# A new order for a two-layer decoder trunk: two DMA queues of unequal shares in the planner, and blocks of 4, 3, 4, 3, 3 tiles

## The chip, the cores and the metric

The kernel runs on the eight cores of one Trainium2 chip. Every core reads all weights from HBM and computes one of eight prompts (2048 tokens) and 16 of 128 sample sequences (8 tokens each, 128 rows); the cores don't talk to each other. The metric is the device time of the slowest core in microseconds (us), the median of several executions. TensorE is called PE in the profile's rows, VectorE DVE, ScalarE ACT, GpSimd POOL, SyncE SP.

## The reference, cut to what matters

```python
def mixer_block(h, ...):                      # both layers
    hn = rms_norm(h, norm_mix)
    proj = hn @ w_in                          # (tokens, 7696)
    q, k, v, g_out, g_lr, xp, u, vv, gates = split(proj)
    g_log = log_sigmoid(g_lr @ w_gk2 + b_gk) / 16        # g_lr has 16 columns
    o, s_new = gla_mix(q, k, v, g_log, s_gla, chunk)     # per head: S = diag(a) S + k^T v, o = q S
    o = rms_norm(o, gla_norm) * silu(g_out)
    branch_a = o @ w_br_a
    pool_out, new_hist = pool_mix(xp, pool_hist, n_prev, w_pool_mix, pool_scale)
    branch_b = pool_out @ w_br_b
    branch_c = spatial_gate(gelu(u), gelu(vv), w_spatial, b_spatial) @ w_br_c
    ga, gb, gc = split(sigmoid(gates))
    return h + (ga * branch_a + gb * branch_b + gc * branch_c) @ w_out, s_new, new_hist, gelu(vv)

def ffn_block(h, ...):
    a = relu(rms_norm(h, norm_ffn) @ w_ff1)
    return h + (a * a) @ w_ff2
```

Model width is 1024, there are 4 heads with keys of 128 and values of 256, the feed-forward width is 4096, and there are two layers. Prompts start from empty states, samples from given ones.

## The kernel before, in words

A core's 2176 rows are 17 tiles of 128 tokens: tile 0 holds the samples, tiles 1 to 16 the prompt. `BLK` groups the tiles into five blocks of 3, 3, 3, 4 and 4. Products that put features on the partitions (k, q, the gates, the first feed-forward matrix) run once for a block, with 384 or 512 columns a matmul, and so need the normed rows of all tiles of their block; v and the second feed-forward matrix run tile by tile. The normed and transposed rows of all tiles stay in SBUF as `hn`.

A layer has these stages: `gla_project` (v, k, q and the low-rank gate, whose 16 columns come from the small matrix `wglr` and go through `wgk2`), `gla_gate` (silu of g_out) and `gla_scan` (the recurrence, tile by tile) for each block; `gla_sample`, the same for 32 pairs of sample and head pair, a generator that stops after certain numbers of them and goes on after the next block; `mix_block` (pooling and spatial gating); `gate_block`, in two halves of the features; `out_block`; and the feed-forward part in four slices, `ff1` and `ff2`. Ahead of the first layer the rows of x are loaded through three buffers `xt`, normed on ScalarE and VectorE, transposed by TensorE and copied to `hn`. The x loads of tiles 6 and up wait until slot 4 of the weight ring has landed (that is the chunk g0).

Weights pass through a ring of seven slots of 8 KB a partition, in the order v0, v1, k, q, g0, g1, xp, u, vv and so on. Each chunk is read as float32 and written as bfloat16 by a DMA on POOL's queue (line 675); the first two chunks, v0 and v1, come in two halves each (line 379), so that TensorE can start on 256 columns. POOL's queue also carries `wglr`, `wgk2` (wgk_bf in the rows), `wpm` and `wsT`. All other transfers (x, states, the vector constants, `bsp` and `rep`, spills and outputs) go through SyncE's queue. Both queues are served by the same 16 DMA engines.

The order of the work on each engine isn't that of the program's text. Every operation is recorded as a node with its reads and writes, an estimated time and latency; `lay_out` then simulates the five engines, the PSUM banks and the two DMA queues, and always takes the node that can start first (by rank where several can). The order that it finds is issued as it stands: an engine that waits on a node waits with all that is queued behind it. So an estimated landing time places matmuls, and it does so blindly. Scan nodes get a lower rank, `LIFT`, which brings them forward. Since helpers record every operation, nearly all matmuls have line 454 (transposes 467), ScalarE's work line 417 and VectorE's lines 425, 428 and 437.

The end of the kernel is `ff2` on the last block, and the last tile's norm and store in halves.

Of the kernel before, what the change touches and what calls it, by code (L numbers as in the profile page):

```python
# [12 lines left out]
KT = 8  # L13
SEQ = 2048
DEPTH = 2
# [8 lines left out]
BLK = [(0, 3), (3, 3), (6, 3), (9, 4), (13, 4)]  # L24
# [122 lines left out]
def build_program():  # L147
# [18 lines left out]
    w_glr = din("w_glr", [DEPTH, 128, KT, 16])  # L166
# [80 lines left out]
    def lay_out(seed):  # L247
# [18 lines left out]
        dma_at = [4000.0] * 5  # L266
# [4 lines left out]
        for _ in range(len(nodes)):  # L271
# [3 lines left out]
            for e in range(5):  # L275
                f = free[e]
                pick = None
                for n in ready[e]:
                    s = rdy[n.idx]
                    if s < f:  # L280
                        s = f
                    if pick is not None and s > pick[0][0] and s > f + 30.0:
                        continue
                    bk = None
                    for b in n.tiles:
                        if kof[id(b)] is None:
                            can = [k for k in b.allowed if bank_of[k] is None]
                            if not can or (len(can) < 2 and b is not tiles_in_order[oldest]):
                                bk = -1
                                break  # L290
                            bk = min(can, key=lambda k: bank_at[k])
                            if bank_at[bk] > s:
                                s = bank_at[bk]
                            break
                    if bk == -1:
                        continue
                    c0 = max(s, f + 30.0)
                    key = key_of[n.idx]
                    if e == 1 and n.aset is not None and n.aset != aset:
                        key += 60  # L300
                        c0 += swap
                    c = (c0, key)
                    if pick is None or c < pick[0]:
                        pick = (c, s, n, bk)
                if pick is not None and (best is None or pick[1] < best[1]):
                    best = pick
            assert best is not None, "no node can be placed"
# [9 lines left out]
            if n.byts:  # L317
                at0 = max(dma_at[e], s + occ)
                other = dma_at[7 - e]
                work = n.byts / (290.0 if e == 3 else 150.0 if dma_at[4] < 20000.0 else 245.0)  # L320
                both = max(0.0, other - at0)
                dma_at[e] = at0 + (both + work - both / 2 if work > both / 2 else work * 2)
                fin = dma_at[e] + (3500.0 if e == 3 else 2500.0)
# [13 lines left out]
            for m in n.succ:  # L337
                j = m.idx
                t = fin + 250.0 if e != 0 or m.E is not PE else fin - n.lat
                if t > rdy[j]:  # L340
                    rdy[j] = t
                need[j] -= 1
                if need[j] == 0:
                    ready[num[id(m.E)]].append(m)
# [17 lines left out]
    class DmaQ:  # L362
# [6 lines left out]
        def dma(self, out, in_, reads=(), writes=(), after=(), turn=False):  # L369
# [15 lines left out]
            if turn:  # L385
                n *= 3
            record(self.E, fn, reads, writes, 500.0 if self.E is SP else 900.0, 0.0, byts=n, after=after)
# [159 lines left out]
    mkb = [24, 30, 36, 42, 50]  # L547
# [103 lines left out]
    def wload(n):  # L651
# [26 lines left out]
        record(POOL, fn, (), [b] + (first[2 * k:2 * k + 2] if n in (NSLOT, NSLOT + 1) else []), 900.0 * len(todo), 0.0, byts=byts)  # L678
# [10 lines left out]
    def setup():  # L689
# [4 lines left out]
        memset(wglr.t[:, :, :], 0.0, [wglr])  # L694
# [18 lines left out]
    def gla_consts(l):  # L713
        plq.dma(wglr.t[:, :, 0:16], w_glr[l], writes=[wglr])
        plq.dma(wgk2.t[:, :], w_gk2[l], writes=[wgk2])

    def mix_consts(l):
        plq.dma(wpm.t[:, :, :], w_pmT[l].rearrange("g d c -> d g c"), writes=[wpm])
        for g in range(4):
            ts(wpm.t[:, g, :], wpm.t[:, g, :], vec_t.t[:, V_PSC + l * 4 + g:V_PSC + l * 4 + g + 1], ALU.mult, [wpm, vec_t], [wpm])  # L720
        spq.dma(bsp.t[:, :, :], b_sp[l:l + 1].broadcast_to([128, 4, 128]), writes=[bsp], after=[slots[6]])

    def mix_prep(l):
        plq.dma(wsT.t[:, :, :], w_spT[l].rearrange("g s t -> s g t"), writes=[wsT], after=[slots[6]])
        spq.dma(rep.t[:, :], rep_d[l], writes=[rep], after=[slots[6]])
# [220 lines left out]
    def gla_sample(l):  # L946
# [11 lines left out]
        for hp in range(2):  # L958
# [8 lines left out]
            for i in range(NSEQ_S):  # L967
# [22 lines left out]
                if n in (5, 15, 25):  # L990
                    yield
# [103 lines left out]
    def gate_block(l, hf, b):  # L1095
# [4 lines left out]
        if b == 0:  # L1100
            for g in range(4):
                ps = psum()
                pe_group([(ps.t[:, :], wpm.t[:, g, :], bbc[1][:, g, :], True, True)], [wpm, bbc[0]], [ps])
                act(bbc[1][:, g, :], ps.t[:, :], AF.Copy, [ps], [bbc[0]])
        for pi, (gw, sw, vw, ktn, src, k0) in enumerate(((ga, ba[0], ba[1], KT, hs, 0), (gb, bbc[0], bbc[1], 4, os_, 0), (gc, bbc[0], bbc[2], 4, os_, 4))):
            for m4 in range(4):
                m = hf * 4 + m4
                psg = hn_fm(b, gw[0], gw[1], m4 * 128)
# [25 lines left out]
    def out_block(l, b):  # L1134
# [8 lines left out]
        for t in tiles(b):  # L1143
            norm_to_hn(t, hB[t].t[:, :], hH[t], hj, hx[t % 2], turn=b >= 2)
# [33 lines left out]
    for t in range(NTILE):  # L1178
        if t == 6:
            wget(0, "g1")  # L1180
        spq.dma(xt[t % 3].t[:, :], rows(x_p, x_s, t), writes=[xt[t % 3]], after=[slots[4]] if t > 5 else ())
        if t == 0:
# [8 lines left out]
            wget(0, "v0")  # L1191
# [113 lines left out]
```

How the kernel before makes its waits and increments, by code:

```python
    def wait(self, tok):  # L43
        if tok is None:
            return
        sem, val = tok
        if sem is self.sem and self.name == "pe":
            return
        k = id(sem)
        if self.seen.get(k, 0) >= val:
            return
        self.e.wait_ge(sem, val)
        self.seen[k] = val
# [1 line left out]
    def tok(self, inst):  # L55
        self.cnt += 1
        inst.then_inc(self.sem, 1)
        return (self.sem, self.cnt)
# [311 lines left out]
            def fn(rs, ws, lt):  # L370
                k = self.i % len(self.sems)
                self.i += 1
                sem = self.sems[k]
                if self.cnt[k] > 0:
                    self.E.wait((sem, 16 * self.cnt[k]))
                acquire(self.E, rs, ws)
                for b in after:
                    self.E.wait(b.w)
                (self.E.e.dma_start_transpose(out=out, in_=in_) if turn else self.E.e.dma_start(out=out, in_=in_)).then_inc(sem, 16)
                self.cnt[k] += 1
                release((sem, 16 * self.cnt[k]), rs, ws)
# [290 lines left out]
        def fn(rs, ws, lt):  # L672
            acquire(POOL, rs, ws)
            for view, src in todo:
                nc.gpsimd.dma_start(out=view, in_=src).then_inc(slot_sem[k], 16)
                slot_cnt[k] += 1
            release((slot_sem[k], 16 * slot_cnt[k]), rs, ws)
```

## Time and profile before

| | |
|---|---|
| time, median of 3 runs | 2383.77 us (2382.52 to 2385.54) |
| the profiled execution's own time | 2381.28 us |
| its span on the slowest core (core 5) | 2380.2 us |
| spans of the eight cores | 2371.6 to 2380.2 us |
| granted TensorE clock, mean | 0.998 |
| TensorE busy | 2323.0 us (98%) |
| VectorE, ScalarE, GpSimd busy | 1273.8, 886.3, 245.9 us |
| DMA moved | 229.41 MB |

The span runs from the first instruction to the last. Busy time of TensorE is modelled for its pipelined matmuls; what is not busy is time in which it had nothing to do. A granted clock of 1.00 is 2.4 GHz, one of 0.50 is 1.2 GHz.

### The profile page before, as it was taken

What the parts mean: (1) busy time and instruction counts of PE and PEld (TensorE: products, weight loads), DVE (VectorE), ACT (ScalarE), POOL (GpSimd) and SP (SyncE); (2) the same over time, 40 slices, a digit from 0 to 9 for tenths busy, and PEclk for the clock granted to TensorE, in tenths of its full rate; (3) what the DMA queues carried; (4) which work ended last, traced back from release to release, by engine and by line L of the source; (5) the groups of instructions that cost most, each with busy time, mean ns of one, the idle gap of its engine ahead of it and who ended that gap; (6) DMA issues with size and microseconds to landing.
All of it is one profiled execution on the core that took longest, in us unless ns stands there. A gap on an engine that the chain in (4) does not pass through costs nothing.

```text
span 2380.2 us, 40912 instructions; the slowest of 8 cores (2371.6 to 2380.2 us)
## 1 busy us (share of the span) xinstructions
PE 2323.0 (98%) x13392; PEld 1236.5 (52%) x13392; DVE 1273.8 (54%) x2231; ACT 886.3 (37%) x1810; POOL 245.9 (10%) x266
## 2 busy tenths in 40 slices
PE   6899999999999999999999999999999999999998
PEld 4576555546445454545455555564554454545453
DVE  3787776444465444434567776744434644434355
ACT  3877753222233121212456678322222421211133
POOL 2123222000000000000012233200000000000000
PEclk9999999999999999999999999999999999999999
DMA  9554936154186040406492467451815642222112
GB/s 162 143 165 122 186 125 142 71 97 111 70 159 103 1 72 1 76 1 116 127 164 74 149 137 157 100 135 63 142 72 107 126 65 36 36 37 36 18 59 93
DMA packets 219415, 229.41 MB, mean 96 GB/s; under 512 B 54315, under 2 KB 203307, under 8 KB 216106
## 3 DMA queue, kind: packets, MB, share of 16 engines
q0 software_dynamic: 83584, 78.45, 23.8%
q1 hardware_dynamic: 135626, 148.35, 20.9%
q8 instruction: 113, 1.85, 0.3%
q14 instruction: 92, 0.75, 0.1%
HBM read 240.41 MB, written 55.05 MB: 124 GB/s over the span
## 4 chain that ended last, share of the span: by engine, by line
PE 91%; DVE 3%; issue 2%; ACT 2%; DMA 2%; POOL 0%; DVEq 0%; ACTq 0%; SPq 0%; POOLq 0%
PE ps L454 90%; DMA wring<-w_in 1%; PE ps L467 1%; DVE U L428 0%; DMA Sf<-sgla 0%; DVE Sf L428 0%; ACT rsg L417 0%; DVE tmp L428 0%; ACT L417 0%; ACT tmp L417 0%; DVE sqg L425 0%; DVE lv L815 0%; ACT Sb L417 0%; DVE pt L425 0%; ACT xj L417 0%
## 5 line engine op out<-in xcount | busy, mean ns | idle before, releaser
L454 PE MATMUL ps<-hn,wring 128*128 128x384 bf16 (+1 forms) x6400 | 1245.4, 347 | 7.8 <-DVE sgt L425 1.7
L454 PEld LDWEIGHTS ps<-hn,wring 128*128 128x128 bf16 x6400 | 621.6, 98 | 545.4 <-issue 13.4
L454 PE MATMUL ps<-wring,a 128*128 128x512 bf16 x2176 | 476.0, 379 | 0.2 <-DVE a L425 0.2
L417 ACT ACTIVATE rl<-ps 128x384 f32<-128x384 f32 (+1 forms) x320 | 169.9, 532 | 637.9 <-PE ps L454 522.2
L425 DVE TENSOR_TENSOR h<-h,ps 128x512 f32<-128x512 f32 x340 | 233.1, 687 | 277.1 <-PE ps L454 276.1
L454 PEld LDWEIGHTS ps<-wring,a 128*128 128x128 bf16 x2176 | 212.8, 98 | 255.1 <-issue 0.7
L425 DVE TENSOR_TENSOR a<-rl 128x384 bf16<-128x384 f32 (+1 forms) x320 | 194.9, 612 | 276.0 <-ACT rl L417 268.0
L417 ACT ACTIVATE sg<-ps 128x384 f32<-128x384 f32 (+1 forms) x240 | 127.9, 533 | 450.3 <-PE ps L454 322.3
L454 PE MATMUL ps<-wring,hn 128*128 128x256 bf16 (+1 forms) x1088 | 193.7, 330 | 12.2 <-DMA wring<-w_in 10.8
L425 DVE TENSOR_TENSOR tmp<-sg,ps 128x384 f32<-128x384 f32 (+1 forms) x160 | 97.3, 608 | 154.4 <-ACT sg L417 79.1
L454 PEld LDWEIGHTS ps<-wring,hn 128*128 128x128 bf16 x1088 | 105.2, 99 | 79.3 <-issue 15.3
L454 PE MATMUL ps<-OBs,wring 128*128 128x384 bf16 (+1 forms) x640 | 143.8, 347 | 0.0
L675 POOL DMA_DIRECT2D wring<-w_ff x32 | 28.0, 875 | 1047.2 <-PE ps L454 1047.2
L425 DVE TENSOR_TENSOR acc<-sg,ps 128x384 f32<-128x384 f32 (+1 forms) x80 | 48.5, 607 | 162.7 <-PE ps L454 162.7
L454 PE MATMUL ps<-H4s,wring 128*128 128x384 bf16 (+1 forms) x640 | 130.7, 347 | 0.0
L454 PE MATMUL ps<-wring,mg 128*128 128x512 bf16 x544 | 119.7, 379 | 0.0
L425 POOL TENSOR_TENSOR go<-tmp,go 128x512 bf16<-128x512 f32 x64 | 77.8, 1221 | 244.4 <-DVE tmp L428 213.0
L417 ACT ACT_TABLE_LOAD x71 | 91.1, 1283 | 26.4 <-PE ps L454 24.2
L454 PEld LDWEIGHTS ps<-H4s,wring 128*128 128x128 bf16 x640 | 62.5, 98 | 55.7 <-issue 0.3
L454 PEld LDWEIGHTS ps<-OBs,wring 128*128 128x128 bf16 x640 | 62.6, 98 | 55.0
L454 PEld LDWEIGHTS ps<-wring,mg 128*128 128x128 bf16 x544 | 52.8, 98 | 61.3
L428 DVE SCALAR_TENSOR_TENSOR tmp<-ps,vec_t,rsg 128x256 f32<-128x256 f32 x136 | 61.7, 477 | 28.6 <-ACT rsg L417 27.5
(137 smaller groups left out, 1777.6 us busy)
## 6 DMA issues: line engine op xcount, KB each, us to landing
wring<-w_ff POOLq DMA_DIRECT2D x32, 1024.0 KB, 13.1
wring<-w_in POOLq DMA_DIRECT2D x28, 1024.0 KB, 16.1
Sf<-sgla SPq DMA_DIRECT2D x64, 256.0 KB, 3.7
gla_s<-Sf SPq DMA_DIRECT2D x64, 256.0 KB, 2.8
H4s<-H_d SPq DMA_DIRECT2D x12, 768.0 KB, 8.5
OBs<-OB_d SPq DMA_DIRECT2D x12, 768.0 KB, 5.0
h_d<-h SPq DMA_DIRECT2D x17, 512.0 KB, 2.7
h<-h_d SPq DMA_DIRECT2D x17, 512.0 KB, 9.9
```

Source lines behind the costliest of these rows:

```text
L417: op(ACT, lambda: nc.scalar.activation(out=now(out), in_=now(in_), func=func, **kw), reads, writes, occ, 125.0, SETS.get(func))
L425: op(E, lambda: E.e.tensor_tensor(out=now(out), in0=now(in0), in1=now(in1), op=alu), reads, writes, occ, 90.0)
L428: op(DVE, lambda: nc.vector.scalar_tensor_tensor(out=now(out), in0=now(in0), scalar=scalar, in1=now(in1), op0=op0, op1=op1), reads, writes ...
L454: inst = nc.tensor.matmul(now(m[0]), m[1], m[2], start=m[3], stop=m[4], **kw)
L467: inst = nc.tensor.transpose(now(o), i, ident_ap)
L675: nc.gpsimd.dma_start(out=view, in_=src).then_inc(slot_sem[k], 16)
```

## The change

The planner's DMA model: before, one finishing time for each queue, with fixed rates and a rough rule for overlap. Now the two queues are simulated as they run. A transfer joins its queue when it is issued, needs its bytes over 300 (SyncE) or 265 (POOL) bytes per ns plus 100 ns, and goes 3 or 1.5 times slower while the other queue has something to move; 2000 ns after its end it has landed, and only then its users become ready. DMA transposes count their bytes once, and take the queue's engine longer.

The data: `wglr` comes from the host padded to 32 columns, so that neither the memset nor the strided write is needed. `wglr` and `wgk2` of the first layer are recorded after v1, not after v0. `bsp` and `rep` wait for the norm of tile 5 (before: for slot 6's last load, which does not exist yet in the first layer, so that they were loaded at once). The x loads wait for slot 4 from tile 7 on, and g1 is requested at tile 7. Blocks are 4, 3, 4, 3, 3 tiles. The sample generator stops after 8, 18 and 28 pairs, before after 6, 16 and 26. The four products that fuse the pooling map into its branch matrix stand two by two ahead of the third and fourth feature tile of the first gated product, before all four ahead of the first. The merged rows `mg` move in SBUF with the block sizes. In `out_block` the tiles from 6 on go through DMA transposes, as before.

```diff
-BLK = [(0, 3), (3, 3), (6, 3), (9, 4), (13, 4)]
+BLK = [(0, 4), (4, 3), (7, 4), (11, 3), (14, 3)]
...
-    w_glr = din("w_glr", [DEPTH, 128, KT, 16])
+    w_glr = din("w_glr", [DEPTH, 128, KT, 32])
...
+            upto = best[1] if best is not None else 1e12
+            while clock < upto and (coming or moving[3] or moving[4]):
+                on = [(moving[3], 3.0 if moving[4] else 1.0), (moving[4], 1.5 if moving[3] else 1.0)]
+                on = [(q, r) for q, r in on if q]
+                to = min([upto] + [clock + q[0][1] * r for q, r in on] + ([max(clock, coming[0][0])] if coming else []))
+                for q, r in on:
+                    q[0][1] -= (to - clock) / r
+                    if q[0][1] < 1e-6:
+                        m = q.popleft()[0]
+                        landing.append((to + m.lat, m.idx))
+                        landing.sort()
+                clock = to
+                while coming and coming[0][0] <= clock:
+                    _, i, e, work = coming.pop(0)
+                    moving[e].append([nodes[i], work])
+                if landing and landing[0][0] < upto:
+                    upto = landing[0][0]
+            if landing and landing[0][0] <= upto:
+                at, i = landing.pop(0)
+                free_up(nodes[i], at)
+                continue
...
             if n.byts:
-                at0 = max(dma_at[e], s + occ)
-                other = dma_at[7 - e]
-                work = n.byts / (290.0 if e == 3 else 150.0 if dma_at[4] < 20000.0 else 245.0)
-                both = max(0.0, other - at0)
-                dma_at[e] = at0 + (both + work - both / 2 if work > both / 2 else work * 2)
-                fin = dma_at[e] + (3500.0 if e == 3 else 2500.0)
+                coming.append((s + occ, n.idx, e, n.byts / (300.0 if e == 3 else 265.0) + 100.0))
+                coming.sort()
...
-            if turn:
-                n *= 3
-            record(self.E, fn, reads, writes, 500.0 if self.E is SP else 900.0, 0.0, byts=n, after=after)
+            record(self.E, fn, reads, writes, 1250.0 if turn else 500.0 if self.E is SP else 900.0,
+                   2000.0, byts=n, after=after)
...
-    mkb = [24, 30, 36, 42, 50]
+    mkb = [24, 32, 38, 46, 52]
...
-        memset(wglr.t[:, :, :], 0.0, [wglr])
...
-        plq.dma(wglr.t[:, :, 0:16], w_glr[l], writes=[wglr])
+        plq.dma(wglr.t[:, :, :], w_glr[l], writes=[wglr])
...
-        spq.dma(bsp.t[:, :, :], b_sp[l:l + 1].broadcast_to([128, 4, 128]), writes=[bsp], after=[slots[6]])
+        spq.dma(bsp.t[:, :, :], b_sp[l:l + 1].broadcast_to([128, 4, 128]), writes=[bsp], after=[hnB[5]])
...
-        spq.dma(rep.t[:, :], rep_d[l], writes=[rep], after=[slots[6]])
+        spq.dma(rep.t[:, :], rep_d[l], writes=[rep], after=[hnB[5]])
...
-                if n in (5, 15, 25):
+                if n in (7, 17, 27):
                     yield
...
-        if b == 0:
-            for g in range(4):
-                ps = psum()
-                pe_group([(ps.t[:, :], wpm.t[:, g, :], bbc[1][:, g, :], True, True)], [wpm, bbc[0]], [ps])
-                act(bbc[1][:, g, :], ps.t[:, :], AF.Copy, [ps], [bbc[0]])
+
+        def fuse(g):
+            ps = psum()
+            pe_group([(ps.t[:, :], wpm.t[:, g, :], bbc[1][:, g, :], True, True)], [wpm, bbc[0]], [ps])
+            act(bbc[1][:, g, :], ps.t[:, :], AF.Copy, [ps], [bbc[0]])
+
...
+                if b == 0 and pi == 0 and m4 > 1:
+                    fuse(2 * m4 - 4)
+                    fuse(2 * m4 - 3)
...
-            norm_to_hn(t, hB[t].t[:, :], hH[t], hj, hx[t % 2], turn=b >= 2)
+            norm_to_hn(t, hB[t].t[:, :], hH[t], hj, hx[t % 2], turn=t > 5)
...
-        if t == 6:
+        if t == 7:
             wget(0, "g1")
-        spq.dma(xt[t % 3].t[:, :], rows(x_p, x_s, t), writes=[xt[t % 3]], after=[slots[4]] if t > 5 else ())
+        spq.dma(xt[t % 3].t[:, :], rows(x_p, x_s, t), writes=[xt[t % 3]], after=[slots[4]] if t > 6 else ())
...
-            wget(0, "v0")
+            wget(0, "v1")
             gla_consts(0)
```

## Rows read from the trace of the kernel before

**Rows 1.** The page's head, and its share of TensorE.

```profile
span 2380.2 us, 40912 instructions; the slowest of 8 cores (2371.6 to 2380.2 us)
...
PE 2323.0 (98%) x13392; PEld 1236.5 (52%) x13392; DVE 1273.8 (54%) x2231; ACT 886.3 (37%) x1810; POOL 245.9 (10%) x266
```

**Rows 2.** Busy time by windows: length, PE, PEld, DVE, ACT, POOL, clock, DMA share, GB/s.

```profile
15.00:20.00 5.00, 2.27 (x14) 1.77 (x15) 0.14 (x2) 0.38 (x2) 0.00 (x0) 1.00 1.04 148
...
35.00:40.00 5.00, 3.57 (x17) 2.49 (x18) 0.20 (x1) 2.67 (x8) 0.00 (x0) 0.50 1.09 132
...
80.00:110.00 30.00, 23.43 (x189) 14.69 (x188) 25.55 (x36) 24.36 (x66) 6.13 (x4) 1.00 0.45 139
...
130.00:400.00 270.00, 260.19 (x1893) 157.69 (x1892) 206.58 (x432) 175.83 (x339) 86.06 (x88) 1.00 0.63 149
1200.00:1480.00 280.00, 269.17 (x1876) 153.57 (x1874) 199.52 (x444) 203.41 (x411) 72.53 (x78) 1.00 0.61 132
```

**Rows 3.** TensorE's waits: for whom, us in total, times, longest.

```profile
PE ps L454 <- DMA wring<-w_in: 10.8, 3, 4.9
```

**Rows 4.** Timeline of POOL's DMA issues: start, duration, instruction.

```profile
3.43 0.87 POOL L379 DMA_DIRECT2D wglr<-w_glr  x1
4.29 0.56 POOL L379 DMA_DIRECT2D wgk_bf<-w_gk  x1
4.84 1.79 POOL L379 DMA_DIRECT2D wring<-w_in  x2
6.58 3.54 POOL L675 DMA_DIRECT2D wring<-w_in  x4
```

**Rows 5.** Timeline of TensorE on core 5: v0's halves, v1's, the first k groups.

```profile
17.73 1.86 PE L454 MATMUL ps<-wring,hn 128*128 128x256 bf16 x8 [4.67 <-DMA wring<-w_in]
...
24.47 1.91 PE L454 MATMUL ps<-wring,hn 128*128 128x256 bf16 x16 [1.27 <-DMA wring<-w_in]
...
36.43 5.16 PE L454 MATMUL ps<-wring,hn 128*128 128x256 bf16 x24 [4.85 <-DMA wring<-w_in]
...
51.05 5.36 PE L454 MATMUL ps<-hn,wring 128*128 128x384 bf16 x32
```

**Rows 6.** DMA issues of 0 to 80 us: count, KB each, median us to landing.

```profile
bsp_p<-b_spatial SPq DMA_DIRECT2D x1, 256.0 KB, 13.7
wgk_bf<-w_gk POOLq DMA_DIRECT2D x1, 128.0 KB, 24.5
...
wglr<-w_glr POOLq DMA_DIRECT2D x1, 32.0 KB, 24.4
```

**Rows 7.** Timeline of TensorE on core 2: the first matmuls on v1.

```profile
30.39 2.78 PE L454 MATMUL ps<-wring,hn 128*128 128x256 bf16 x24 [2.76 <-DMA wring<-w_in]
```

**Rows 8.** Span and clock of core 2.

```profile
core 2: 2371.6 us, clock 0.999
```

**Rows 9.** Weight slots issued 5.7 to 7.4 us (v1's right half, k): landing.

```profile
DMA to landing us min/median/max: 34.5/37.7/41.0
```

**Rows 10.** Timeline of SyncE's queue: the x loads of tiles 6 to 14.

```profile
61.42 37.58 SPq L379 DMA_DIRECT2D xt<-xp  x9
```

**Rows 11.** Timeline of VectorE: tile 5's copy to hn.

```profile
46.08 0.69 DVE L437 COPY hn<-ps 128x1024 bf16<-128x1024 bf16 x1 [0.51 <-PE ps L467]
```

**Rows 12.** The chain that ended last, its last ReLU and square.

```profile
2358.72 0.60 ACT rl L417
...
2359.42 0.70 DVE a L425
```

**Rows 13.** VectorE's groups by form: count, busy us, mean ns, idle before.

```profile
L428 DVE SCALAR_TENSOR_TENSOR tmp<-ps,vec_t,rsg 128x256 f32<-128x256 f32 x136 | 61.7, 477 | 28.6 <-ACT rsg L417 27.5
L428 DVE SCALAR_TENSOR_TENSOR Sf<-Sf,eblS,ps 128x256 f32<-128x256 f32 x128 | 58.7, 472 | 9.0 <-PE ps L454 8.7
L428 DVE SCALAR_TENSOR_TENSOR U<-U,eblP,ps 128x256 f32<-128x256 f32 x128 | 55.2, 473 | 10.4 <-PE ps L454 10.3
...
L428 DVE SCALAR_TENSOR_TENSOR xn<-xt,ssq,wn 128x1024 bf16<-128x1024 f32 x17 | 21.5, 1280 | 18.3 <-ACT ssq L417 13.6 <-ACT wn L417 4.6
```

More of the change, by code:

```diff
@@ L1 @@
+import collections
 import numpy as np
@@ L265, in lay_out @@
         aset = None
-        dma_at = [4000.0] * 5
+        clock = 4000.0
+        coming = []
+        moving = {3: collections.deque(), 4: collections.deque()}
+        landing = []
         order = []
@@ L270, in lay_out, with free_up @@
                 ready[num[id(n.E)]].append(n)
-        for _ in range(len(nodes)):
+        def free_up(n, fin):
+            for m in n.succ:
+                j = m.idx
+                t = fin + 250.0 if n.E is not PE or m.E is not PE else fin - n.lat
+                if t > rdy[j]:
+                    rdy[j] = t
+                need[j] -= 1
+                if need[j] == 0:
+                    ready[num[id(m.E)]].append(m)
+        while len(order) < len(nodes):
             while oldest < len(tiles_in_order) and id(tiles_in_order[oldest]) in opened:
@@ L336, in lay_out @@
             order.append(n)
[L337 to L344, printed above, removed]
+            if not n.byts:
+                free_up(n, fin)
         return max(free), order, kof
@@ L677, in fn @@
             release((slot_sem[k], 16 * slot_cnt[k]), rs, ws)
-        record(POOL, fn, (), [b] + (first[2 * k:2 * k + 2] if n in (NSLOT, NSLOT + 1) else []), 900.0 * len(todo), 0.0, byts=byts)
+        record(POOL, fn, (), [b] + (first[2 * k:2 * k + 2] if n in (NSLOT, NSLOT + 1) else []), 900.0 * len(todo), 2000.0, byts=byts)
         views[order[n][0]] = [b] + vs
@@ L1274 @@
     gk2 = gk2.reshape(DEPTH, 128, 512)
-    glr = np.ascontiguousarray(f(w_in)[:, :, C_GLR:C_GLR + 16].reshape(DEPTH, KT, 128, 16).transpose(0, 2, 1, 3))
+    glr = np.zeros((DEPTH, 128, KT, 32), np.float32)
+    glr[:, :, :, 0:16] = f(w_in)[:, :, C_GLR:C_GLR + 16].reshape(DEPTH, KT, 128, 16).transpose(0, 2, 1, 3)
     w8 = np.swapaxes(f(w_spatial)[:, :, 0:8, 0:8], 2, 3).transpose(0, 2, 1, 3).reshape(DEPTH, 8, 32)
```

## The prediction

> **What bounds the kernel now.** I began with the page: TensorE (PE) is busy 2323.0 of 2380.2 us [rows 1], so at most 57 us can come from idle PE; the matrix work is that of the same seventeen tiles either way. The second view is busy time by windows, and it says where the 57 us lie [rows 2]: from 80 to 110 us PE misses 6.6 us, from 130 to 400 us 9.8, from 1200 to 1480 us 10.8, and a five-microsecond window at the start can be half empty (2.27 of 5 at 15 to 20 us). The page's rows of the branch and feed-forward stages hold no idle worth naming, so they can't be shortened by an order. Third, who PE waited for: the largest entry by far is the transfer of a weight slot, 10.8 us in only three waits, the longest 4.9 us [rows 3]. All three are in the first 37 us.
>
> The fourth view places them [rows 4, 5]. The two first weight chunks come in halves. PE starts on the left half of v0 at 17.73, on its right half at 24.47 and on the left half of v1 only at 36.43 us. v0's halves are 6.7 us apart, v1's first half comes 12.0 us after v0's last. Between those issues on POOL's queue stand wglr (issued at 3.43) and wgk2 (4.29). By their times to landing [rows 6], wglr is in at 3.43 + 24.4 = 27.8 and wgk2 at 4.29 + 24.5 = 28.8 us: 3.4 us for 32 KB, then 1.0 us for 128 KB. wglr is 1024 runs of 64 bytes of the source. In the wait that follows PE's granted clock falls to half: 0.50 at 35 to 40 us, which is 1.2 instead of 2.4 GHz [rows 2], and the first 24 matmuls on v1 take 5.16 us [rows 5].
>
> Fifth, is a microsecond of the start worth one at the end? Two cores that run the same program answer that. Core 2 gets v1 at 30.39 us and its 24 matmuls take 2.78 us, not 5.16 [rows 7]. It is 6.0 us earlier and saves 2.4 us of slow clock, 8.4 us together; its span is 2371.6 against 2380.2 us, 8.6 us less [rows 1, 8]. So what the slowest core gains before 40 us it keeps.
>
> **The change part by part.** wglr and wgk2 move behind v1's two halves. v1's left half follows v0's right half directly: 28.8 - 24.5 = 4.3 us earlier. Bounds: nothing, if the gap has another cause, and 12.0 - 6.7 = 5.3 us, if v1 follows at the pace of v0's halves. I take 4.3, as it is what the two landings show.
>
> The padded wglr is one contiguous run of 1 KB in each partition, 128 runs for 1024. At the price of a run in the old load, 3.4 us become 0.4, so all that is behind it gains 3.0 us more or less for good. That counts for k: it lands now at 6.6 + 41.0 = 47.6 us [rows 4, 9], and its first matmul group starts at 51.05 [rows 5], with no wait. After: k in at 47.6 - 3.0 - 0.9 = 43.7, wanted at 51.05 - 6.4 = 44.7 (both subtractions follow from this paragraph's terms and the next two). It still holds, with 1 us to spare; if that cover goes, at most the difference is lost. wglr itself will be there about a microsecond after v1's right half, and its chain (gate, exponentials, scan) needs some 5 us of ScalarE and VectorE before the k groups can be drained: covered by the v work of four tiles. The removed memset is off every path.
>
> bsp and rep now wait for tile 5's norm: bsp's 256 KB [rows 6] and rep's 16 (128 x 32 float32) leave the transfers ahead of v0's landing. At 148 GB/s, the rate in a window where the DMA engines are full [rows 2], that is 1.9 us of transfer. Both queues share it, so v0 gains between 0 and 1.9; I take 0.9. They are wanted only by the branch stage hundreds of microseconds later. In the second layer the same two wait for an earlier event than now, which costs nothing. What is queued behind them on SyncE are the loads of x from tile 6 on; those stand until 61.42 us at present [rows 10], and tile 5's copy to hn begins at 46.08 [rows 11], so no x load is later.
>
> Clock: with v1 at about 31 us the slowest core would be where core 2 is, and keep the full clock; but at half speed it would lose 2.4 us as now. I can't tell from which idle the clock falls, so I take 1.2, bounds 0 and 2.4.
>
> Block 0 of four tiles, and tile 6 free of the wait for g0: PE has seven tiles' work before it needs the gated ones, not six. That can only be won from the 6.6 idle us between 80 and 110, where VectorE is busy 25.55 of 30 us [rows 2]. As VectorE's work there is not less, I take 0.5, bounds 0 and 3.3 (half the idle).
>
> The last block has three tiles: at the very end PE waits for one ReLU (0.60) and one square (0.70 us) at 512 columns [rows 12]; at 384 they cost three quarters at best: 0.3 less.
>
> Portions 8, 10, 10, 4, the later fuse groups, the DMA model, the byte count of transposes: they alter the order alone. PE waits nowhere in the gate stage, so fuse is free either way. In the two scan stages the idle is 3.6% and 3.9% of the time [rows 2] although their orders differ; that difference is 1.3 us over both. I take 0 and allow 3 us either way.
>
> Sum: 4.3 + 0.9 + 1.2 + 0.5 + 0.3 = 7.2 us. The profiled execution took 2381.28 us, 1.1 more than its span, and lies 2.5 below the median of 2383.77. 2381.3 - 7.2 = 2374.1 for such an execution, 2376.6 us for the median.
>
> **The rivals.** First, the small loads don't hold the queue. v1's half also competes with x copies, and its right half lands at about 5.7 + 34.5 = 40.2 [rows 4, 9], only some 4 us after the left: the pace of halves is not constant, so the 12.0 us gap may be the x copies' doing. Against it: wglr's own 3.4 us. Then the first and the clock term vanish and 0.9 + 0.5 + 0.3 = 1.7 us are left: 2382.1. The Trainium skill speaks for this rival, in DMA: Bandwidth & Descriptors, Anatomy of one DMA: of a transfer's cost about 2 us are fixed and "dominated by completion latency, not setup latency", and the rest is bytes at 436 GB/s. By that page, an estimate: 160 KB would hold what is behind them 0.4 us, and the sum would be 0.4 + 1.7 = 2.1 us instead of 7.2. The trace disagrees so far: the landings of [rows 6] are 3.4 and 1.0 us apart from what came before.
>
> Second, the gain is won and lost again: everything up to 75 us comes 6 us earlier, but tiles 7 to 16 are normed no faster, and PE waits in 80 to 125 us for what VectorE can't give sooner. Against it: cores 2 and 5 keep their distance through that window. It leaves about 2 us: 2381.8.
>
> Third, slower. The place is VectorE at 80 to 125 us. Block 0's third prompt tile brings its scan forward (four updates of U and four of tmp, 3.8 us at 0.473 and 0.477, and half as much again, by estimate, for its masks, copies and squares: 5.7); two more samples bring 4 x 0.472 = 1.9 [rows 13]; block 2's wide groups need tile 10, not tile 8: two more norms of 1.28 and their copies to hn, some 4 us. 11.6 us of VectorE work is pulled into a stretch that has 4.5 idle us in 30. If all the rest, 7 us, and the same again on ScalarE reached PE, 14 - 7.2 = 7 us would be lost: 2390.6. It decides from 12 us on (7.2 won plus the 4.8 that can be told). For it: both engines are near full there. Against it: block 2's wide groups start at 115 us at present, when tile 10 is long done.
>
> **How the numbers follow.** 0.2% of this kernel, 4.8 us, is about what a measurement can tell: faster is under 2379.0, slower over 2388.5. The forecast has 0.62, the first rival 0.12, the second 0.12, the third 0.14. The forecast ends inside 4.8 us in a few of its cases (clock term 0 and order term +3), the second rival is a touch faster in as many. So faster 0.61, same 0.26, slower 0.13. Likeliest 2376.6. All gains at their bounds, 5.3 + 1.9 + 2.4 + 3.3 + 0.3 + 3, are 16.2 us: 2368 at the low end. The high end takes in the two rivals near 2382 with order's 3 us, and not the third: 2386. The forecast's own range is 2371 to 2381.
>
> **What would show it.** v1's first matmul on the slowest core at 30 to 32 us and its three waits for weight slots down from 10.8 to under 7; wglr landing within 1.5 us of v1's right half; the clock at 1.00 through 40 us; spans of all eight cores shorter by like amounts, and the window 80 to 110 at 6 idle us or fewer. If v1's half is still 12 us behind v0's, the first rival holds; if v1 is early and PE's idle from 80 to 125 has grown by 5, the second or third. The prediction is wrong in any case if PE shows a new wait of several microseconds in the scan stages, which no row of before can exclude.

## The result, and the profile after

The changed kernel takes 2395.77 us (median of 6 runs; 6 runs of the kernel before beside it: 2383.8). The ratio is 1.0047, with an interval of 1.0033 to 1.006: slower by about half a per cent, where 0.3% faster had been forecast. A few executions of several kernels below were disturbed, by tens to hundreds of microseconds; the ratios leave these out and the medians don't, so ratios are given. The profiled execution took 2396.22 us. The spans of its eight cores are 2381.4 to 2395.1 us, 2388.1 on average, and those of the kernel before averaged 2376.0: every core is longer, by 3 to 24 us. That is one execution of each. Over all the executions that the ratios use, the mean core takes 2388.6 us here and 2377.4 to 2378.6 in the kernel before, so the profile of before is on the short side and the loss is rather 10 to 11 us than 12.

The head of the page of the changed kernel, and its share of TensorE, beside [rows 1]:

```profile
span 2395.1 us, 40873 instructions; the slowest of 8 cores (2381.4 to 2395.1 us)
...
PE 2332.3 (97%) x13392; PEld 1240.1 (52%) x13392; DVE 1276.9 (53%) x2230; ACT 861.9 (36%) x1792; POOL 243.3 (10%) x266
```

The same 13392 matmuls take 9 us more and the idle is 62.8 us for 57.2. So it is both idler and, at times, slower. The windows of core 2, the slowest, in the order of the columns of [rows 2], show in which stages. The first four are windows of [rows 2], which are those of core 5:

```profile
35.00:40.00 5.00, 4.43 (x46) 3.04 (x44) 2.26 (x3) 2.50 (x8) 0.00 (x0) 1.00 1.11 184
...
80.00:110.00 30.00, 23.82 (x194) 16.69 (x192) 24.05 (x39) 24.88 (x62) 5.67 (x4) 0.86 0.46 131
130.00:400.00 270.00, 259.87 (x1896) 159.75 (x1895) 198.26 (x408) 160.10 (x328) 81.65 (x84) 0.99 0.61 138
1200.00:1480.00 280.00, 272.13 (x1872) 153.41 (x1870) 199.97 (x432) 200.94 (x413) 71.56 (x78) 1.00 0.64 138
...
700.00:800.00 100.00, 94.78 (x485) 45.42 (x483) 58.66 (x78) 33.16 (x83) 1.75 (x2) 0.98 0.59 90
1880.00:2000.00 120.00, 115.75 (x569) 55.05 (x567) 61.84 (x86) 30.55 (x68) 1.75 (x2) 0.97 0.34 54
```

The scan stage of the second layer has become better (7.9 us idle for 10.8). The last two windows are new to the story: 5.2 and 4.2 us idle at the passage from the output product to the feed-forward part, once in each layer. Before, a core had 0.1 us idle there on average.

One table serves for all that follows. For each kernel and stretch it gives, averaged over the eight cores, TensorE's idle time and, behind the stroke, the time that its slow clock cost (busy time by one minus the granted clock), both added up from windows of five microseconds:

```
                     0-60       60-130    130-400    700-800   1200-1540  1880-2000
before             17.2/1.6    7.0/0.0   10.1/0.0    0.1/0.0   11.2/0.0    0.1/0.0
after              17.6/0.2    9.3/2.6    9.8/1.8    3.8/0.9    8.9/0.4    2.7/1.0
e1_turn3           17.5/0.2    9.6/2.5    9.4/1.5    0.1/0.0    9.3/0.4    0.1/0.0
e9_databack        21.9/1.1    7.5/2.1    9.9/0.2    0.1/0.0    9.1/0.3    0.1/0.0
e11_pad            16.2/1.0    7.1/0.6   10.4/0.0    0.1/0.0   12.4/0.3    0.1/0.0
e12_bsplate        15.1/2.1    7.9/0.2   11.4/0.6    0.1/0.0   10.9/0.0    0.1/0.0
e13_pad_bsplate    13.6/0.9    8.4/1.1   10.7/0.0    0.1/0.0   11.3/0.0    0.1/0.0
e8_turn1           17.1/1.2    6.9/0.2   10.7/0.0    6.5/2.1   11.6/0.1    4.6/1.9
e5_share           19.5/2.0    7.6/1.5   13.9/2.0    0.7/0.0    8.9/0.0    0.4/0.0
```

After less before, over all six columns, is 6.4 us of idle and 5.3 of clock, 11.7 together; the spans are longer by 12.1 on average. So these columns hold the loss. 8.2 of it lie in the two passages.

TensorE's waits on core 2, in the columns of [rows 3], name the new one: VectorE's squares `a`, twice, 5.2 us the longest. The wait for weight slots fell from 10.8 to 7.2 us (forecast: under 7).

```profile
PE ps L480 <- DVE a L451: 9.5, 2, 5.2
PE ps L480 <- DMA wring<-w_in: 7.2, 3, 3.8
```

The chain of work through the first passage, on the same core (start, us, what), tells what held the squares:

```profile
743.01 9.40 DMA hn<-hx
...
752.50 1.30 DVE hx L454
...
753.89 11.74 DMA hn<-hx
...
765.71 0.61 ACT rl L443
...
766.48 0.70 DVE a L451
767.18 0.14 issue
767.32 32.81 PE ps L480 x154
```

A DMA transpose of one tile's normed rows takes 9.40 us to land; its buffer `hx` is only then free for the next tile, whose transpose takes 11.74 us; and behind that stands a ReLU on ScalarE. The ReLU doesn't read the transposed rows. It writes `rl0`, whose bytes (24 to 26 KB of the partition) are those of the second `hx` buffer, so it must wait until tile 15's transpose has read them. ScalarE's timeline shows what that does to the rest, in the columns of [rows 5]:

```profile
756.67 0.60 ACT L443 ACTIVATE rl<-ps 128x512 f32<-128x512 f32 x1 [1.13 <-PE ps L480]
765.71 1.08 ACT L443 ACTIVATE rl<-ps 128x512 f32<-128x512 f32 x2 [8.44 <-DMA hn<-hx]
```

8.44 us of waiting in an engine that takes its work in order. In the changed kernel this ReLU is sixth of the feed-forward part's; in the kernel before, the first nine all use the other three buffers.

VectorE's order has the same fault. The norm of the last tile, which writes the first `hx` buffer, stands ahead of the squares of the fourth and fifth ReLU (754.95 and 756.67 us) and waits for the transpose that was issued at 744.8:

```profile
762.11 1.28 DVE L454 SCALAR_TENSOR_TENSOR hx<-h,ssq,wn 128x1024 bf16<-128x1024 f32 x1 [7.12 <-DMA hn<-hx]
763.31 1.29 DVE L451 TENSOR_TENSOR a<-rl 128x512 bf16<-128x512 f32 x2
```

So two engines are held by slow transposes, and TensorE by both. The ReLU's wait is the one that ends last.

### The profile page after: what moved, and what is told of

The parts are those of the page before. It is cut to its first block, busy times and chain, and to the rows that moved or that the text cites. A ratio compares the mean times of both kernels' runs of the same rounds, so it can differ in the third digit from the quotient of the medians.

```text
span 2395.1 us, 40873 instructions; the slowest of 8 cores (2381.4 to 2395.1 us)
## 1 busy us (share of the span) xinstructions
PE 2332.3 (97%) x13392; PEld 1240.1 (52%) x13392; DVE 1276.9 (53%) x2230; ACT 861.9 (36%) x1792; POOL 243.3 (10%) x266
## 4 chain that ended last, share of the span: by engine, by line
PE 89%; DMA 4%; DVE 2%; issue 2%; ACT 1%; another core or an unknown queue 0%; POOL 0%; SPq 0%; DVEq 0%; ACTq 0%; POOLq 0%
PE ps L480 89%; DMA hn<-hx 2%; DMA wring<-w_in 1%; PE ps L493 1%; DMA Sf<-sgla 1%; DMA xt<-xp 1%; DMA gla_s<-Sf 0%; ACT L443 0%; DVE tmp L454 0%; DVE lv L840 0%; ACT rsg L443 0%; DVE Sf L454 0%; DVE U L454 0%; DVE hx L454 0%
## 5 line engine op out<-in xcount | busy, mean ns | idle before, releaser
L443 ACT ACT_TABLE_LOAD x53 | 68.0, 1283 | 25.3 <-PE ps L480 23.3
```

Source lines behind the costliest of these rows:

```text
L443: op(ACT, lambda: nc.scalar.activation(out=now(out), in_=now(in_), func=func, **kw), reads, writes, occ, 125.0, SETS.get(func))
```

## The experiments

In the short diffs a minus is a line of the kernel that each starts from, which is named.

**e1_turn3.** The changed kernel with the old one's `if turn` restored: a DMA transpose counts its bytes three times in the planner.

```diff
+            if turn:
+                n *= 3
```

> The changed kernel with one line more in the planner: a DMA transpose again counts three times its bytes. Nothing that is computed or moved is altered, only the order. In the changed kernel ScalarE's ReLU into rl0, whose bytes are those of hx1, stands sixth in its queue behind tile 15's transpose, and TensorE loses 3 to 5 us at 700 to 800 us and 1 to 5 us at 1880 to 2000 us. In this kernel that ReLU no longer stands among the first nine. Theory A (the transposes' price in the planner costs the two transitions): both windows at 0 to 1 idle us, time 5 to 11 us below the changed kernel, 2385 to 2391. Rival (the stalls come from the blocks of 4, 3, 4, 3, 3, which let ff2 of block 0 stand earlier): the windows keep 3 us or more each and the time stays within 3 us of 2396.

Measured: median 2384.65 us, ratio to the kernel before 1.0005 (0.9995 to 1.0015); spans 2377.6 to 2382.2 us. The two passages, on its slowest core, 6:

```profile
700.00:800.00 100.00, 100.00 (x516) 48.36 (x515) 60.63 (x82) 33.22 (x83) 1.76 (x2) 1.00 0.56 86
1880.00:2000.00 120.00, 120.00 (x598) 57.98 (x595) 60.77 (x88) 31.93 (x70) 1.75 (x2) 1.00 0.32 51
```

No idle and no slow clock. The spans fall by 8.5 us on average, the median by 11. In the table no number outside the two passages changes by more than half a microsecond, and TensorE's order is that of the changed kernel, instruction for instruction, until 763 us (compared on core 5). Equal to the kernel before holds for the slowest core; the mean core takes 2379.9 us over the ratio's executions, for 2377.4.

**e8_turn1.** The same from the other side: the kernel before without those two lines, and nothing else.

```diff
-            if turn:
-                n *= 3
```

> The kernel before with one edit: a DMA transpose counts its bytes once in the old planner. Theory A (the price of a transpose alone makes the stalls at the two transitions, in whatever model and blocks): the ReLU into rl0 stands fifth or sixth and waits for tile 15's transpose, TensorE idles 2 to 5 us at 700 to 800 us and as much at 1880 to 2000, nothing else moves, 2389 to 2394. Rival (the stall needs the new model's blocks or shares): no idle in these windows, within 2 us of 2384.

Measured: ratio 1.0072 (1.0057 to 1.0087), spans 2387.6 to 2401.6 us. The passages on core 5, and ScalarE's timeline in the first:

```profile
700.00:800.00 100.00, 93.07 (x502) 47.56 (x500) 55.48 (x79) 30.01 (x72) 1.75 (x2) 0.97 0.43 71
1880.00:2000.00 120.00, 116.70 (x600) 57.87 (x599) 63.68 (x90) 34.13 (x80) 1.75 (x2) 0.97 0.28 52
```

```profile
747.86 0.49 ACT L415 ACTIVATE rl<-ps 128x384 f32<-128x384 f32 x1 [0.81 <-PE ps L452]
758.42 0.87 ACT L415 ACTIVATE rl<-ps 128x384 f32<-128x384 f32 x2 [10.07 <-DMA hn<-hx]
```

The same stall, of 10.07 us here, with the old blocks, the old DMA model and the old data. TensorE's order is that of the kernel before until 753.8 us, and in the table the two passages lose 14.9 us of the 17.0 by which the mean span grows. The price of the transposes alone makes it. What this price moves is both the ReLU and the norms of the last tiles; no run moves one without the other.

**e2_consts.** The kernel before with all the moves of data (`wglr` padded and with `wgk2` behind v1, `bsp` and `rep` behind tile 5), under the old planner and blocks.

```diff
-        plq.dma(wglr.t[:, :, 0:16], w_glr[l], writes=[wglr])
+        plq.dma(wglr.t[:, :, :], w_glr[l], writes=[wglr])
...
-        spq.dma(bsp.t[:, :, :], b_sp[l:l + 1].broadcast_to([128, 4, 128]), writes=[bsp], after=[slots[6]])
+        spq.dma(bsp.t[:, :, :], b_sp[l:l + 1].broadcast_to([128, 4, 128]), writes=[bsp], after=[hnB[5]])
...
-            wget(0, "v0")
+            wget(0, "v1")
             gla_consts(0)
```

> The kernel before with only the data moves: wglr padded and without memset, wglr and wgk2 behind v1, bsp and rep behind tile 5's norm. Old planner, old blocks. Theory A (the forecast's first terms are right by themselves: v1's left half is in at 25 to 31 us instead of 30 to 36 on every core, and what is won before 40 us is kept): 3 to 8 us less than before, 2376 to 2381. Rival (the gain at the start is lost again by 130 us): v1 as early, but the time within 2 us of 2384.

Measured: median 2392.35 us, ratio 1.0039 (1.0021 to 1.0057). The start has less idle, but on cores 4 to 7 the stretch of 60 to 130 us has 3.5 to 5.3 us more of it and loses 2.7 to 5.6 us of clock. Neither theory had room for that: the time is above the kernel before, by 9 us. And k is no longer covered: its first group waits on TensorE, on core 5 and, most, on core 7:

```profile
42.19 5.36 PE L454 MATMUL ps<-hn,wring 128*128 128x384 bf16 x32 [0.99 <-DMA wring<-w_in]
```

```profile
45.52 4.75 PE L454 MATMUL ps<-hn,wring 128*128 128x384 bf16 x20 [3.87 <-DMA wring<-w_in]
```

So the moves of data, which I had credited with the whole gain, don't bring it under the old planner, whose order they also change.

**e3_oldblk.** The changed kernel with the blocks of before (and the offsets and tile numbers that go with them).

```diff
-BLK = [(0, 4), (4, 3), (7, 4), (11, 3), (14, 3)]
+BLK = [(0, 3), (3, 3), (6, 3), (9, 4), (13, 4)]
```

> The changed kernel with the old blocks of 3, 3, 3, 4, 4 (and mg's places, the g1 request and the x loads' wait from tile 6 as before). If the blocks are what costs time between 80 and 120 us (15 of 20 us busy at 100 to 120 in the changed kernel, 18 in the one before), that window is back at 17 to 18 busy us and the time is 3 to 7 us below the changed kernel, 2389 to 2393. If the planner's model is what costs it, the time stays within 3 us of 2396. The stall at 700 to 800 us stays in either case, since the ReLU into rl0 still stands early.

Measured: ratio 1.0177 (1.0162 to 1.0192), 42 us. The idle of 130 to 400 us is 20.6 us on the mean core, 9.8 in the changed kernel, spread over many waits of a microsecond or so (none over 1.7 on the slowest core), and the clock costs 5.8 us there for 1.8; both passages keep their stalls. The forecast of 3 to 7 us less is refuted, as is its rival.

**e4_planner.** The kernel before with only the planner replaced (the queue simulation, the latency of 2000 ns, the transposes' price).

```diff
+                on = [(moving[3], 3.0 if moving[4] else 1.0), (moving[4], 1.5 if moving[3] else 1.0)]
...
-            if turn:
-                n *= 3
```

> The kernel before with only the new planner model (two queues with shares, transposes counted once, 2000 ns to land). Blocks, data and waits of before. If the model alone explains the loss: 2391 to 2397, with 3 to 5 idle us at 700 to 800 us, the same again at 1880 to 2000. If only the transposes' price does harm: 2386 to 2391. If the blocks were the cause: within 2 us of 2384.

Measured: median 2420.94 us, ratio 1.0157 (1.0144 to 1.0171). Much the picture of e3: on the mean core 19.8 us idle at 130 to 400 us and 4.4 and 4.2 us in the passages. On core 1 one wait of 5.0 us, for ScalarE's `xptok`, stands out in that stretch. The two runs together say that the blocks and the planner can't be priced one by one: with the new planner the old blocks cost 31 us (e3 against the changed kernel), and yet with its own planner they are as good as the new blocks are with theirs (the kernel before, and e1). Both runs count a transpose once; the old blocks under the new model with the threefold price were not run.

**e5_share.** e1 with SyncE's slowdown beside POOL's queue at 1.5 in place of 3.0, so that the planner expects the x loads earlier and places tile 1's transposes ahead of v0's right half, as the kernel before does.

```diff
-                on = [(moving[3], 3.0 if moving[4] else 1.0), (moving[4], 1.5 if moving[3] else 1.0)]
+                on = [(moving[3], 1.5 if moving[4] else 1.0), (moving[4], 1.5 if moving[3] else 1.0)]
```

> e1_turn3 with one number changed in the planner: SyncE's queue goes 1.5 times slower, not 3 times, while POOL's moves something. In e1_turn3 and in the changed kernel tile 1's transposes stand on TensorE behind the products with v0's right half (20 us), although its x rows are in by 12; its copy to hn begins at 24.4 us on core 5 (20.6 before). Here the transposes of tile 1 stand ahead of all products. Theory A (the planner's low share for SyncE makes TensorE miss what the early weights bring): tile 1's hn by 17 us, idle TensorE at 0 to 60 us down from 17 to 12 to 14 us on all cores, and if that is kept to the end, 3 to 5 us below e1_turn3, 2379 to 2382. Rival (what is won before 60 us is lost at 60 to 130): idle falls in the first window and rises in the second, time within 2 us of e1_turn3.

Measured: median 2391.38 us, ratio 1.003 (1.0017 to 1.0044). The transposes stand where they should, but the table has 2.0 us more idle and 1.8 more clock in the first 60 us than e1, 3.0 less of both from 60 to 130, and 5.0 more from 130 to 400. So the loss lies behind the place that was changed. My theory that this one place cost the start its gain is refuted, and the rival's picture isn't seen either: another order has other waits.

**e6_jit_before and e7_jit_e1.** Is the difference of two orders anything more than chance? A small jitter on the ranks (0 to 4, against ties) gives another order from the same planner, for the kernel before and for e1.

```diff
-        swap = 400.0 if seed == 0 else float(rng.integers(0, 1300))
+        swap = 400.0
...
-        _, order, kof = min((lay_out(seed) for seed in range(ORDERS)), key=lambda r: r[0])
+        _, order, kof = min((lay_out(seed) for seed in (1,)), key=lambda r: r[0])
```

> The kernel before with ranks of the planner jittered by up to 4 places (its own option, another seed). Nothing else changes. It shows how much two equally reasoned orders of the same work differ. If orders were all as good, within 2 us of 2384. If the kernel before holds a lucky order: 5 to 20 us slower.

> e1_turn3 with the same jitter of ranks as e6_jit_before. If the new model plans better, its orders vary less: within 4 us of e1_turn3. If e1's 2384.65 is as much luck as before's: 5 to 20 us slower.

Measured: 1.0225 (1.0211 to 1.0238) and 1.0207 (1.0193 to 1.022), 54 and 49 us. It was not a mild shuffle. TensorE's timeline of the jittered kernel before has the largest cause, on core 6:

```profile
79.70 1.01 PE L467 MATMUL ps<-ident_bf,xn 128*128 128x128 bf16 x8 [23.01 <-DVE xn L428]
```

Transposes of tiles whose x loads wait for slot 4 were placed ahead of block 1's products, and TensorE stood 23.01 us behind them, within 38.5 us of such waits from 60 to 130 us. On the mean core the stretch has 38.6 us idle for 7.0 and loses 8.5 us of clock; e7 has 36.4 and 8.2 there, and 20.6 and 7.2 from 130 to 400 us. The two runs don't give the scatter of ordinary orders, which I wanted. They do show what a single misplacement costs.

**e9_databack.** e1 with the data of before: `wglr` narrow, with `wgk2` behind v0, `bsp` and `rep` at once. What is left of the change is then the planner, the blocks, the portions and the smaller moves.

```diff
-            wget(0, "v1")
+            wget(0, "v0")
             gla_consts(0)
```

> e1_turn3 (changed kernel, transposes priced three times) with the data of the kernel before: 16 columns of wglr with the memset, wglr and wgk2 between v0 and v1, bsp and rep at once. If the data moves are worth what the forecast gave them (4.3 + 0.9 and the clock), this is 4 to 7 us slower than e1_turn3, near 2390. If the moves only shift the idle time from the first 60 us into the next 70 (e1_turn3 has 8 to 12 idle us and 1 to 4 us of slow clock there, before 7 and none), then 60 to 130 goes back to 7 and none, and the time is within 3 us of e1_turn3.

Measured: median 2387.0 us, ratio 1.001 (1.0 to 1.002). By the ratios that is 1.2 us over e1, the second outcome of the two, though 60 to 130 us keeps 2.1 us of clock. In the table: 0 to 60 us has 5.3 us more of idle and clock than e1, which is what the moves of data win there, with the order that the planner makes of them (TensorE's differs from 37.6 us on). Against the kernel before, the new order alone costs 4.2 us in this stretch and 2.6 in the next, and wins 1.8 in the second layer's scan.

**e11_pad, e12_bsplate, e13_pad_bsplate.** The kernel before with `wglr` padded in its old place; with `bsp` and `rep` late; with both. All three leave TensorE's order as it was, row by row, so these are the only runs in which transfers move and that order doesn't. (VectorE's and ScalarE's differ in a few places.)

```diff
-        plq.dma(wglr.t[:, :, 0:16], w_glr[l], writes=[wglr])
+        plq.dma(wglr.t[:, :, :], w_glr[l], writes=[wglr])
```

```diff
-        spq.dma(rep.t[:, :], rep_d[l], writes=[rep], after=[slots[6]])
+        spq.dma(rep.t[:, :], rep_d[l], writes=[rep], after=[hnB[5]])
```

> The kernel before with wglr padded to 32 columns and no memset, in its old place between v0 and v1. TensorE's order is that of before, row by row, so that only the transfer differs. Forecast's price: 1024 runs become 128, 3.0 us off POOL's queue, so v1's left half is in 3 us earlier on every core. If an early start is kept: 2.5 to 3.5 us less than before, up to 5 with the slow clock, 2379 to 2382. Rivals: a small load doesn't hold the queue, or the gain is lost by 130 us: within 1.5 us of before.

> The kernel before with bsp and rep behind tile 5's norm, nothing else; TensorE's order is that of before. Forecast: v0's left half 0.9 us earlier (0 to 1.9), time 1 us less. In the changed kernel v0 was there 3.1 us earlier on core 5, so by that: 2 to 4 us less, 2380 to 2382. Rival: the bytes only move to 50 us, where the queue is as full, and k, q and g0 come as late as before: within 1 us.

> e11_pad and e12_bsplate together: both moves that leave TensorE's order as it is. If the two add up and are kept: the sum of the two gains, 4 to 7 us below before, 2377 to 2380, faster than both kernels of the study. If TensorE then waits for k (in at about 43 us) or for tile norms: no better than the larger of the two.

Measured: ratios 0.9993 (0.9983 to 1.0004), 0.9997 (0.9987 to 1.0007) and 1.0006 (0.9981 to 1.003). With both, v1's first matmul starts at 29.4 us on the mean core, for 32.9 before, and the first 60 us win 4.3 us of idle and clock. From 60 to 130 us 2.5 of them are lost again. The ratios show no gain, but they don't exclude one of a few microseconds. One execution of 2405.94 us makes e13's interval wide; the other six of its ratio take 2380.2 to 2385.8 us, with the median of before beside them at 2384.5. On the mean core, over the executions of the ratios, e11 is 2.7 us shorter than before, e12 0.4 and e13 0.9 (2.2 without that one). Core 5 of e13 is the case that my argument from two cores had in mind: span 2370.0 us, for 2380.2 before. But core 3's is 2379.5, and that core sets the time.

## Why the prediction was wrong

**The step that failed** is the one on the order: "they alter the order alone ... I take 0 and allow 3 us either way". The term turned out the largest of all, and a loss. The transposes' price alone is worth 8.5 us on the mean core and 11 in the median (e1), and put into the kernel before it costs 17 us (e8). From 7.2 us won to 11 lost is 18 us: 11 are these passages, and the other 7 are the forecast's gains, of which nothing reaches the slowest core in e1, the change without them. I had read two stages for what an order could do there, both scan stages with many small waits, and carried their 1.3 us to the whole kernel. The loss came in a passage where no row of before shows idle, because its order was right: a queue in order has no small price for one misplaced instruction.

**How it works** can be followed in numbers, and this part is shown: e1 and e8 alter this price alone. By the diff, the planner gives a tile of 256 KB over 300 bytes per ns, plus 100 ns and 2000 ns, 3.0 us to land, and 4.9 with POOL's queue busy. The trace has most of them at just that, but not those in the passage. SyncE's transposes of 690 to 800 us on core 2, and then, each alone, the three issued at 743.0, 744.8 and 753.9:

```profile
DMA to landing us min/median/max: 3.0/3.2/17.2
```

```profile
DMA to landing us min/median/max: 9.4/9.4/9.4
```

```profile
DMA to landing us min/median/max: 17.2/17.2/17.2
```

```profile
DMA to landing us min/median/max: 11.7/11.7/11.7
```

With the threefold bytes the plan was 4.7 us alone and 10.2 beside the other queue. That figure is false for a transpose in quiet, and nearly right for those that matter. It is not that the transposes got slower: in the kernel before the slowest of this stretch takes 13.4 us, in e1 17.7, and TensorE waits for none of them: no ReLU of the passage waits for a transpose there, and the norms that wait for one hold back nothing that TensorE needs.

**Why they are slow there** is shown by coincidence, not by a run. Two weight chunks of 1 MB are issued on POOL in just that time:

```profile
743.20 0.87 POOL L701 DMA_DIRECT2D wring<-w_ff  x1 [58.20 <-PE ps L480]
744.92 0.88 POOL L701 DMA_DIRECT2D wring<-w_ff  x1 [0.85 <-PE ps L480]
```

The transposes issued from 720 us until then land in 3.0 to 4.8 us, and the last one, at 763.5, in 3.1 again. The share that each queue has of the 16 DMA engines' time says the same. From 743 to 766 us POOL's queue (q0) has 70.0%; from 720 to 743 it has no row, and SyncE's (q1) is all but alone:

```profile
q0 software_dynamic: 2080, 2.10, 70.0%
```

```profile
q1 hardware_dynamic: 7536, 2.36, 60.3%
```

It holds for all 304 DMA transposes of the changed kernel's eight cores, counted from its trace. The 207 with no packet of POOL's queue between issue and landing take 3.0 to 5.0 us, 3.1 in the median. The 70 in whose time that queue has 40% or more of the DMA engines take 6.2 to 21.8, 12.2 in the median. The kernel before has 204 and 69 of them, with 3.0 to 4.8 and 6.1 to 18.8 us. The Trainium skill says in DMA: Bandwidth & Descriptors, Issuing engines are not separate DMA queues, that transfers run on the same 16 DMA engines and interleave, whichever engine starts them; the trace agrees with it, by the 70.0% above, but no run here moved the chunks away.

**The transfers** did as forecast, or better. TensorE on core 5 begins v0's halves at 14.65 and 19.90 us, v1's left half at 25.28 (forecast 30 to 32), for the 17.73, 24.47 and 36.43 of [rows 5]:

```profile
14.65 1.87 PE L480 MATMUL ps<-wring,hn 128*128 128x256 bf16 x8 [1.38 <-DMA wring<-w_in]
...
19.90 1.86 PE L480 MATMUL ps<-wring,hn 128*128 128x256 bf16 x8 [3.38 <-DMA wring<-w_in]
...
25.28 5.32 PE L480 MATMUL ps<-wring,hn 128*128 128x256 bf16 x32 [2.66 <-DMA wring<-w_in]
```

So the first rival, that the small loads don't hold the queue, fell for the two together. For the padding alone the runs are nearer to it: v1 comes 1.0 us earlier on the mean core in e11, where 3.0 had been my term, and two executions with the same transfers differ by 0.4 (before 32.9, e8 33.2). In the changed kernel v1 is 7.6 us earlier on the mean core (25.3 for 32.9). Its issue is about 1.5 us sooner, as no small load is issued ahead of it, and `bsp` and `rep` account for 1.8 in e12. The Trainium skill's account in DMA: Bandwidth & Descriptors, Anatomy of one DMA, by which, as an estimate, 160 KB would have held the queue only 0.4 us, doesn't fit the 5.8 us that are left, or 4.3 without the earlier issue. No run moves `wglr` and `wgk2` behind v1 with the order held, so their share and the padding's stay apart only by e11.

The smaller terms: v0 gains 2.0 us on the mean core from `bsp` and `rep` alone (e12: 14.8 for 16.8), where I took 0.9 and had 1.9 as the bound. The first k group, with no wait, stands by k's cover (46.65 us on core 5, k forecast for 43.7); under the old planner's order (e2) that cover is gone, as its 3.87 us show. The 0.5 us for block 0 and the 0.3 for the end are too small to be told here.

**"What the slowest core gains before 40 us it keeps"** failed too. v1 is 7.6 us earlier on the mean core, yet the first k group starts there at 46.5 us, 46.8 before. The new order puts tile 0's products with v0's right half ahead of tile 1's transposes, so tile 1 is late. Its copy to `hn`, on core 5 before and after (in e1 it starts at 24.38):

```profile
20.56 0.69 DVE L437 COPY hn<-ps 128x1024 bf16<-128x1024 bf16 x1 [5.42 <-PE ps L467]
```

```profile
22.73 0.69 DVE L463 COPY hn<-ps 128x1024 bf16<-128x1024 bf16 x1 [7.46 <-PE ps L493]
```

And where the order is held fixed (e13), over half of the gain is given back by 130 us. The comparison of two cores was not a fluke: on all eight cores of the kernel before a later v1 goes with a longer span (30.4 to 31.6 us with 2371.6 to 2374.8, 33.7 to 36.4 with 2377.5 to 2380.2). But e13 brings v1 3.4 us forward on the mean core, and its spans average 2375.4 us for 2376.0. So what differs between cores of one execution doesn't price a transfer that is moved. How much of such a gain the mean core keeps stays open, since e11 has 2.7 us less for 1.0 us of v1.

The second rival, which I had given 0.12, has the outcome right and the place wrong. It had TensorE wait from 80 to 125 us; in e13 the idle grows at 60 to 80 us (3.6 us on the mean core for 1.7, clock 0.95 for 1.00), and from 80 to 125 it is 4.8 for 5.2. It had not counted the clock either, which is the greater half of what the changed kernel loses from 60 to 130 us (2.6 us, and 2.3 of idle). My clock term was right at the start (1.00 from 35 to 40 us, 1.4 us won on the mean core, though core 5 has 0.66 from 25 to 30) and missed that the same cost can turn up later.

**The third rival**, VectorE as the new bound from 80 to 125 us, gave 2390.6 us, the nearest number. Its mechanism is there, at a smaller price. From 100 to 120 us, core 5 before and core 2 after:

```profile
100.00:120.00 20.00, 17.06 (x138) 11.26 (x137) 13.16 (x17) 15.71 (x38) 2.56 (x2) 1.00 0.38 119
```

```profile
100.00:120.00 20.00, 15.06 (x110) 9.80 (x111) 19.07 (x33) 13.77 (x38) 1.18 (x2) 0.83 0.47 136
```

VectorE is busy 19.07 of 20 us for 13.16, and what TensorE waits for most from 80 to 130 us is its work: copies to `hn` (4.5 us) and norms (1.9). On the mean core, from 80 to 125 us, VectorE's busy time rises from 33.9 to 38.6 us and TensorE's idle from 5.2 to 8.0, where the rival had 14 us reach TensorE. The two cores chosen hide this from 80 to 110 us (6.2 us idle for 6.6), because core 5 had the most idle of all before. That the rival's number is near is luck all the same, as 8.2 us of the loss lie in the passages, which it doesn't have. e1 keeps this stretch as it is (38.4 and 8.1) and is equal to the kernel before. The clock falls with it: 0.83 beside 4.9 us idle in these 20, before 1.00 beside 2.9. Which of the waits caused it I can't say.

**What adds up:** on the mean core the passages cost 8.2 us, the clock of 60 to 400 us 4.4, the idle of 60 to 130 us 2.3; the second scan stage gives 1.9 back and the start 1.0. 130 to 400 us is idle 0.3 less. That is 11.7 of the spans' 12.1.

**What stays open:** why the old blocks suffer so under the new planner (e3, e4; 130 to 400 us, where in e3 no single wait stands out), which share each small order difference has, and how wide chance orders scatter. No kernel here beats the one before by more than its interval. e1 is the best form of the change that was run, and equal to it on the slowest core.

## What to carry to other kernels

Where a planner writes out the order, a cost in it is a part of the kernel: judge a change of one by which instruction it can move in front of which, and look in the stages where the engines show no wait at all, since there one misplaced instruction shows up whole. Look above all at buffers that share bytes with something a DMA still reads, and price that DMA by its slowest landing beside other traffic rather than by its median. And a gain at the start counts only if the next stage that waits on something else lets it through: hold the order fixed and measure that first. Compare the mean over the cores as well as the slowest one, since the slowest core of one kernel isn't that of another.

## What the hardware showed that I had not expected

A DMA transpose of one tile lands in 3.0 to 5.0 us while POOL's queue moves nothing (207 of 304 in the changed kernel) and takes 6.2 to 21.8 us when that queue has 40% or more of the DMA engines' time, and it is as slow where TensorE doesn't wait for it (13.4 us before, 17.7 in e1). Padding 16 columns to 32, for an eighth of the runs and twice the bytes, moved what stood behind it by 1.0 us on average and not by 3. TensorE's clock fell to a mean of 0.97 in both passages of e8 beside 6.9 and 3.3 us of idle. From 80 to 110 us of the changed kernel it was 0.86 on core 2 with 6.2 us idle in 30, where core 5 of the kernel before kept 1.00 with 6.6; the sum of idle over such a stretch didn't tell what the clock would be.
